# Weights asked for ahead of a stage's end, and h read back by ranges of tokens, in a two-block float32 network on one core

## The chip, the cores and the metric

The kernel runs on one core of one Trainium2 chip. Its time is device microseconds of one execution; the median of several runs is given. The engines are PE (matrix multiply), DVE (vector), ACT (scalar), POOL (general) and SP, which here only issues transfers. All five run their own instruction streams and meet by semaphores.

## The reference

Two transformer-like blocks over 1024 tokens of width 1024, with 256 context tokens before them, all in float32. The first block mixes a gated delta rule (GDN) and retention, multiplies each by a silu gate, projects, and ends with a gated feed-forward part. The second has a state-space branch and two attention branches, each multiplied by a sigmoid gate and merged.

```
h = concat([modulate(rms_norm(ctx)), modulate(rms_norm(x))])      # 1280 tokens x 1024
p = h @ w_in                                                      # qkv, z, ab | rq, rk, rv, rg
o_gdn = rms_norm(o_f + o_b) * silu(z)                             # "gate 1"
rq, rk = rope(rq), rope(rk) * d**-0.5
o_ret = group_norm(r_f + r_b) * silu(rg)                          # "gate 2"
x = x + g1 * (concat([o_gdn, o_ret]) @ w_out)                     # first output projection
x = x + g2 * swiglu(modulate(rms_norm(x)))
# second block
m = sigmoid(ga)*(ya @ w_oa) + sigmoid(gb)*(ys @ w_ob) + sigmoid(gc)*(yc @ w_oc)
x = x + gate1 * (m @ w_out_2);  x = x + gate2 * conv_ffn(...)
```

## The kernel before

The program is a row of stages in a fixed order, the same on every engine: GDN projections and scan (`gp`, `gs`), gate 1 (`gg1`), retention projections (`rp`), retention scan (`rs`), means and gate 2 (`rg`, `gg2`), first output projection (`op1`), first feed-forward (`ffn1`), state space (`sx`, `sc_`, `sz`), merge 0, attention 1 with merge 1 (`att1`, `mg1`), attention 2 with merge 2 (`att2`, `mg2`), second output projection and feed-forward. At the start of a stage an engine passes `barrier(e, stage)`, which waits until all engines have finished what the stage before counts on its semaphores, since the SBUF of one stage is given to the next.

Activations lie with the width on the partitions: h is 8 blocks of 128 rows by 1280 tokens, one after another in a partition, with the context tokens first. The latent tokens are worked on in two ranges, `LAT = [(0, 512), (512, 512)]`; over all tokens the ranges are `ALL = [(0, 256), (256, 512), (768, 512)]`. h is 5 MB and is stored to HBM (`hspill`) in the first stage. It is read back into SBUF twice: for gate 1 and the retention projections (`hT2`), and for gate 2 (`hT3`), at the same address; both transfers are issued by POOL, after the barrier.

Weights come in blocks of 256 columns (1 MB with 8 blocks of 128 rows) into two slots, `wslot0` and `wslot1`, taken in turn. `load()` on SP waits until the slot is given back by the last reader of its former block (`slots.give`), and then issues. SP goes through all loads and stores of the kernel in program order, so a wait on SP holds everything behind it, and a barrier that stands ahead of a load holds the load.

In a gate (`Gate`) PE first does the sums of squares of a head (`norm`), then for each of 4 tiles of 128 columns and both token ranges 8 products of h with weights; ACT applies silu, DVE multiplies. In gate 1 and `rp` each tile also carries a piece of the adaLN modulation (`at1`: weights asked for by POOL, multiplied by POOL, reduced by DVE, summed by PE). In `rp`, PE does a tile, and one tile later rotates its copy, which ACT has taken out of PSUM (`raw`); ahead of its first copy ACT computes decay tables. `op1` uses weights and activations split into a high and a low part (`woh`, `wol`, `op1yh`, `op1yl`): ACT writes the high part, DVE the rest; PE does three products for each. DVE waits for x (`x1_in`) when it has split y, and before it splits the second column of weights.

In attention each of two head groups (`AttGroup`) computes 8 gate tiles beside its scores and stores them to HBM (`gspill`, on SP, each when ACT has copied it); the merge reads them back (`gr`), applies the sigmoid and multiplies them with the branch's products. Merges 1 and 2 have 4 weight blocks "o" of 512 KB each.

Of the kernel before, what the change touches and what calls it, by code (L numbers as in the profile page):

```python
# [96 lines left out]
def build(nc, io, out):  # L97
# [238 lines left out]
    class Ada:  # L336
# [7 lines left out]
        def sp(self, e, g):  # L344
            load(e, (self.nm, g), [(self.w, 0, 8, g * 256, 256, 0)])
# [1147 lines left out]
    class Gate:  # L1493
# [41 lines left out]
        def pe(self, e):  # L1535
            st = self.st

            def norm(x):
                for n0, n in LAT:
                    b = self.bk.take("norm", x, n0)  # L1540
                    for ev in self.bk.freed("norm", x, n0):
                        e.wait_ge(*ev)
                    e.wait_ge(*st.act.after("sq", x, n0))
                    e.matmul(b[:, 0:n], ones, self.sq[:, self.at(x, n0, n)]).then_inc(st.pe("norm", x, n0), 1)
            norm(0)
            for ev in self.ready:
                e.wait_ge(*ev())
            for m in range(4):
                e.wait_ge(*loaded(self.nm, m // 2))
                s = slots[self.nm, m // 2]  # L1550
                for n0, n in LAT:
                    b = self.bk.take("mm", m, n0)
                    for ev in self.bk.freed("mm", m, n0):
                        e.wait_ge(*ev)
                    product(e, b[:, 0:n], [(wtile(s, k, m % 2 * 128), self.h(k, CT + n0, n)) for k in range(8)]).then_inc(st.pe("mm", m, n0), 1)
                    if self.tiles:
                        self.tiles.pe(e, m * 2 + n0 // 512)
                    if n0 == 0 and m < 3:
# [35 lines left out]
    drop(m0)  # L1594
    drop(m2, "right")
    hT2 = sb("hT2", [8 * TT])
    h2_in = Sem("hT2", 16)
    (hb, hbc) = views(hT2)
    bk_r = Ring(bank)
    at1 = AdaTiles("at1", [(ad1, m, 0) for m in range(16, 40)], bk_r, [sb(f"at1w{i}", [1024]) for i in range(3)])  # L1600
    mg = mark()
    gg1 = Gate("gate1", 1536, hb, yg, "gdn_norm_g", lambda x, n0: [], [lambda: h2_in.after("in")])
    gg1.bk, gg1.tiles = bk_r, at1
    drop(mg)

    def gate1_sp(e):
        gg1.sp(e)
# [13 lines left out]
    def gate1_pool(e):  # L1621
        barrier(e, gs)
        e.wait_ge(*hs_out.after("out"))
        e.dma_start(hT2[:, :], io["hspill"]).then_inc(h2_in("in"), 16)
        at1.pool(e, range(9))


# [14 lines left out]
    RT = [(0, m, n0, n) for m in range(4) for n0, n in ALL[1:]] + [(1, m, n0, n) for m in range(4) for n0, n in ALL]  # L1642

    def rp_sp(e):
        barrier(e, gg1.st)
        e.dma_start(rope1[:, :], io["rope1"]).then_inc(rope1_in("in"), 16)
        for g in range(6):
            load(e, ("rqkv", g), [(w1, 0, 8, RQ + g * 256, 256, 0)])

    def rp_dst(kind, m, n0, n):  # L1650
# [4 lines left out]

    def rp_pe(e):
        barrier(e, gg1.st)
        e.wait_ge(*h2_in.after("in"))

        def rotate(t):  # L1660
            kind, m, n0, n = t
# [282 lines left out]
    yr = rb("yr", [4 * NL])  # L1944
    m3 = mark()
    hT3 = sb("hT3", [8 * TT])
    h3_in = Sem("hT3", 16)
    (hd3, _) = views(hT3)
    rg = Stage("rg", rp)
    gg2 = Gate("gate2", 3600, hd3, yr, "ret_norm_g", lambda x, n0: [rg.dve.after("c", x, n0)], [lambda: h3_in.after("in")])  # L1950
    bk_g = gg2.bk
    drop(m0)

# [26 lines left out]

    def rg_pool(e):
        barrier(e, rs)
        e.dma_start(hT3[:, :], io["hspill"]).then_inc(h3_in("in"), 16)


    rsx = sb("rsx", [NL])
# [120 lines left out]
    class OutProj:  # L2107
# [6 lines left out]
            self.bk = Ring(bank[0:6])  # L2114
            self.xs = halves(self.yh, self.yl)

        def sp(self, e):
            for g in range(4):
                load(e, (self.nm, g), [(self.w, 0, 8, g * 256, 256, 0)])

        def cut_act(self, e, j):
# [69 lines left out]
    drop(0, "right")  # L2191

    def op1_sp(e):
        barrier(e, gg2.st)
        e.dma_start(x1[:, :].rearrange("p (k t) -> p k t", t=NL), io["xT"]).then_inc(x1_in("in"), 16)
        op1.sp(e)

    def op1_act(e):
        barrier(e, gg2.st)
# [975 lines left out]
    class Merge:  # L3175
# [10 lines left out]

        def sp(self, e):
            if self.att:
                for x in self.att.g_out:
                    e.wait_ge(*x.now())  # L3190
                barrier(e, *self.before)
            for g in range(4):
                if self.att:
                    for m, n0, n in self.blocks[g * 4:g * 4 + 4]:
                        gb = self.gr.take(m, n0)
                        for ev in self.gr.freed(m, n0):
                            e.wait_ge(*ev)
                        e.dma_start(gb[:, 0:n], io["gspill"][:, m * NL + n0:m * NL + n0 + n]).then_inc(self.gate_in(m, n0)(self.br, m, n0), 16)
                    load(e, (self.nm, "o", g), [(self.wo, 0, self.kt, g * 256, 256, 0)])
                else:  # L3200
                    for q in (0, 1) if g == 0 else (g + 1,) if g < 3 else ():
                        load(e, (self.nm, "g", q), [(w2, 0, 8, self.col + q * 256, 256, 0)])
                    load(e, (self.nm, "o", g), [(self.wo, 0, self.kt, g * 256, 256, 0)])

        def tiles_pe(self, e, kind, g, there=lambda n0: []):
            st, bk = self.st, self.bk
# [78 lines left out]
    class AttGroup:  # L3285
# [85 lines left out]
            e.activation(b[:, :], self.bg[m, n0][:, :], AF.Copy).then_inc(self.st.act("g", m, n0), 1)  # L3371
            self.bg.give((m, n0), self.st.act.now())

        def gate_sp(self, e):
            for b in range(8):
                m, n0 = self.gate(b)
                if b == 4:
                    load(e, (self.nm, "g", m // 2), [(w2, 0, 8, self.at.gcol + m * 128, 256, 0)])
                e.wait_ge(*(self.sj if b < self.early else self.st).act.after("g", m, n0))
                out_ = self.at.g_out[b % 3]  # L3380
                e.dma_start(io["gspill"][:, m * NL + n0:m * NL + n0 + 512], self.gs[m, n0][:, :]).then_inc(out_(self.at.br, m, n0), 16)
                self.gs.give((m, n0), out_.now())


        def sp(self, e):
            g = self.g
            load(e, (self.nm, "k"), [(w2, 0, 8, self.at.k0 + 64 * g, 64, 64 * x) for x in range(2)])
            load(e, (self.nm, "q"), [(w2, 0, 8, self.at.q0 + g * 256, 256, 0)])
            load(e, (self.nm, "g", g * 2), [(w2, 0, 8, self.at.gcol + g * 512, 256, 0)])
            self.gate_sp(e)  # L3390

        def lags(self, j):

# [314 lines left out]
    class Attention:  # L3708
# [19 lines left out]
        def yk(self, k, n0, n):  # L3728
            return self.y[:, k * NL + n0:k * NL + n0 + n]

        def sp(self, e):
            load(e, ("v", self.br), [(w2, 0, 8, self.v0, 128, 0)])
            for gr in self.groups:
                gr.sp(e)

        def pe(self, e):
            barrier(e, *self.before)
# [138 lines left out]
    def sp(e):  # L3876
        a_sp(e)
        gp_sp(e)
        gs_sp(e)
        gate1_sp(e)  # L3880
        rp_sp(e)
        rg_sp(e)
        op1_sp(e)
        ffn1_sp(e)
        fn_sp(e)
        sx[0].sp(e, 0)
        sx[0].sp(e, 1)
# [11 lines left out]
        op2.sp(e)  # L3899
        ffn2.sp(e)  # L3900
        last_sp(e)

# [164 lines left out]
```

## Time and profile before

| | before |
|---|---|
| median of 3 runs | 4852.59 us (4849.14 to 4853.21) |
| the profiled execution's own time | 4851.07 us |
| its span in the trace | 4849.1 us |
| PE busy | 4374.9 us, 90% of the span |
| mean granted clock of PE | 0.948 of full |
| DVE, ACT, POOL busy | 2341.2, 1394.8, 965.8 us |
| chain that ended last | PE 61%, DVE 9%, ACT 5%, DMA 1% |

The span is what the trace covers; the profiled execution took 2.0 us more than it. Times below are microseconds from the span's start. The time in brackets behind a row of a timeline is how long the engine had stood idle before it, and who released it.

### The profile page before, as it was taken

How to read it: one execution, taken by the hardware profiler on the slowest of the kernel's cores; microseconds unless marked ns; L12 is line 12 of the kernel's file. 1: busy time of each engine (PE TensorE's matmuls, PEld its weight loads, DVE VectorE, ACT ScalarE, POOL GpSimd, SP SyncE). 2: the span in 40 equal slices, each digit the busy share in tenths (PEclk: the TensorE clock that was granted, in tenths of full speed). 3: DMA queues.
4: the chain of work that ended last, by engine and by line, in shares of the span. 5: the costliest groups of instructions: out<-in, count | busy, mean ns of one | idle time of the engine just before them, and what ended most of it. 6: DMA issues, size and time to landing. Idle time of an engine off the chain costs nothing.

```text
span 4849.1 us, 45136 instructions
## 1 busy us (share of the span) xinstructions
PE 4374.9 (90%) x18128; PEld 3029.8 (62%) x18128; DVE 2341.2 (48%) x3763; ACT 1394.8 (29%) x2615; POOL 965.8 (20%) x743
## 2 busy tenths in 40 slices
PE   7895789988999999988889998989888888999998
PEld 3454754756788888645554455555564647888886
DVE  2768974252555563335442017563666644333334
ACT  2462221122211111332311005351453532222222
POOL 0114634121344441025241000002000011000001
PEclk9997899999999999988889999999999999999999
DMA  5112233112233431120211110112000031111111
GB/s 187 36 63 72 81 124 108 38 44 87 79 113 109 122 109 48 67 71 27 70 34 35 36 43 22 31 48 61 20 20 16 20 112 37 53 44 50 46 44 61
DMA packets 253617, 301.47 MB, mean 62 GB/s; under 512 B 18992, under 2 KB 209856, under 8 KB 251872
## 3 DMA queue, kind: packets, MB, share of 16 engines
q1 hardware_dynamic: 234976, 216.66, 14.6%
q0 software_dynamic: 15312, 76.68, 5.0%
q10 hardware_dynamic: 3120, 5.24, 0.3%
q8 instruction: 143, 2.34, 0.2%
q14 instruction: 66, 0.54, 0.0%
HBM read 268.47 MB, written 30.09 MB: 62 GB/s over the span
## 4 chain that ended last, share of the span: by engine, by line
PE 61%; DVE 9%; ACT 5%; DMA 1%; issue 1%; POOL 1%; SPq 0%; POOLq 0%; DVEq 0%; ACTq 0%
PE bank L193 59%; PE bank L196 2%; DVE Mx L205 1%; ACT Mx L202 1%; ACT at21P L202 1%; ACT at20P L202 1%; DVE at21sm L223 1%; POOL sq L205 1%; DVE at20sm L223 1%; DVE x L211 0%; DMA wslot<-in_w_in 0%; DVE wfl L205 0%; DVE at11sm L223 0%; DMA hT<-hspill 0%; DVE at21Pl L205 0%
## 5 line engine op out<-in xcount | busy, mean ns | idle before, releaser
L193 PE MATMUL bank<-h,wslot 128*128 128x512 f32 (+3 forms) x2096 | 899.5, 573 | 32.9 <-DMA wslot<-in_w_in 19.2
L193 PEld LDWEIGHTS bank<-h,wslot 128*128 128x128 f32 (+1 forms) x2096 | 383.8, 191 | 378.7 <-issue 361.2
L193 PE MATMUL bank<-hT,wslot 128*128 128x512 f32 (+3 forms) x1136 | 466.0, 567 | 36.6 <-DMA hT<-hspill 20.1
L193 PEld LDWEIGHTS bank<-hT,wslot 128*128 128x128 f32 (+1 forms) x1136 | 213.7, 191 | 264.7 <-issue 237.9
L193 PE MATMUL bank<-ffn1h,wfh 128*128 128x512 f32 x704 | 280.0, 398 | 11.4 <-DVE ffn1l L211 10.6
L193 PE MATMUL bank<-ffn2h,wgh 128*128 128x512 f32 x704 | 276.5, 393 | 9.7 <-DVE ffn2l L211 9.2
L211 DVE SCALAR_TENSOR_TENSOR x<-bank,mod,x 128x512 f32<-128x512 f32 x224 | 164.4, 746 | 247.0 <-PE bank L193 246.7
L193 PE MATMUL bank<-ffn1l,wfh 128*128 128x512 f32 x704 | 275.3, 391 | 0.0
L193 PE MATMUL bank<-ffn2l,wgh 128*128 128x512 f32 x704 | 274.9, 390 | 0.0
L193 PE MATMUL bank<-ffn1h,wfl 128*128 128x512 f32 x704 | 274.7, 390 | 0.0
L193 PE MATMUL bank<-ffn2h,wgl 128*128 128x512 f32 x704 | 274.7, 390 | 0.0
L205 DVE TENSOR_TENSOR wfl<-wslot,wfh 128x1024 fp32r<-128x1024 f32 (+2 forms) x92 | 151.0, 1642 | 149.6 <-ACT wfh L202 149.6
L205 POOL TENSOR_TENSOR ffn2al<-ffn2ga,ffn2ah 128x512 fp32r<-128x512 f32 x44 | 57.4, 1305 | 655.3 <-ACT ffn2ah L202 655.3
L226 DVE TENSOR_REDUCE at2a<-ffn1t 128x128 f32<-128x1024 f32 x72 | 143.1, 1988 | 44.2 <-POOL ffn1t L205 44.2
L193 PEld LDWEIGHTS bank<-ffn1h,wfh 128*128 128x128 f32 x704 | 132.6, 188 | 44.2 <-DVE ffn1l L211 10.2
L193 PEld LDWEIGHTS bank<-ffn2h,wgh 128*128 128x128 f32 x704 | 132.5, 188 | 43.2 <-DVE ffn2l L211 10.2
L211 DVE SCALAR_TENSOR_TENSOR ffn2ga<-ffn2gw,par,ffn2ga 128x1024 f32<-128x1024 f32 x44 | 56.5, 1285 | 199.5 <-ACT ffn2ga L202 198.7
L205 POOL TENSOR_TENSOR sq<-sq 128x512 f32<-128x512 f32 x56 | 71.7, 1280 | 397.0 <-ACT sq L202 395.1
L193 PEld LDWEIGHTS bank<-ffn1h,wfl 128*128 128x128 f32 x704 | 132.8, 189 | 28.0
L193 PEld LDWEIGHTS bank<-ffn2h,wgl 128*128 128x128 f32 x704 | 132.7, 189 | 27.7
L193 PEld LDWEIGHTS bank<-ffn2l,wgh 128*128 128x128 f32 x704 | 132.7, 189 | 26.8
L193 PEld LDWEIGHTS bank<-ffn1l,wfh 128*128 128x128 f32 x704 | 132.9, 189 | 25.4
(533 smaller groups left out, 8867.6 us busy)
## 6 DMA issues: line engine op xcount, KB each, us to landing
wslot<-in_w_in SPq DMA_DIRECT2D x40, 1024.0 KB, 5.5
ffn1t<-in_w_mod POOLq DMA_DIRECT2D x64, 512.0 KB, 4.8
wslot<-in_w_ffn_in SPq DMA_DIRECT2D x44, 512.0 KB, 5.4
Mx<-acsT SPq DMA_DIRECT2D x32, 512.0 KB, 4.9
at1w<-in_ada_w POOLq DMA_DIRECT2D x24, 512.0 KB, 4.6
wslot<-in_ffn_w_gate SPq DMA_DIRECT2D x22, 512.0 KB, 4.0
wslot<-in_ffn_w_up SPq DMA_DIRECT2D x22, 512.0 KB, 5.3
hT<-hspill POOLq DMA_DIRECT2D x2, 5120.0 KB, 15.3
```

The lines of the kernel that those rows point to most:

```text
L193: return Counted() if counting[0] else self.q.matmul(o, l, r, start=start, stop=stop)
L196: return Counted() if counting[0] else self.q.transpose(o, i, ident)
L202: return Counted() if counting[0] else self.q.activation(o, i, f, **k)
L205: return Counted() if counting[0] else self.q.tensor_tensor(o, a, b, op)
L211: return Counted() if counting[0] else self.q.scalar_tensor_tensor(o, a, s, b, op0, op1)
L223: return Counted() if counting[0] else self.q.reduce_max(o, a, AX.X)
L226: return Counted() if counting[0] else self.q.reduce_sum(o, a, AX.X)
```

## The change

Five edits. (1) h is read back in one transfer for each range of tokens, each with a semaphore of its own, the ranges of latent tokens first; the gates' PE waits for a range only when it comes to it, and the second reading leaves the context tokens out. (2) In `rp_sp` the first two weight blocks are asked for ahead of the barrier and of the table of cosines. (3) In `op1_sp` two of four blocks are asked for ahead of the barrier and of x. (4) In an attention, the next user's first block (the key weights of the second head group, or the merge's first block) is asked for ahead of the store of the seventh gate tile. (5) The merge asks for its second block before it waits for the stores and the barrier.

```diff
 class Gate, pe():
             norm(0)
-            for ev in self.ready:
-                e.wait_ge(*ev())
             for m in range(4):
                 e.wait_ge(*loaded(self.nm, m // 2))
                 s = slots[self.nm, m // 2]
                 for n0, n in LAT:
+                    e.wait_ge(*self.ready(n0))
                     b = self.bk.take("mm", m, n0)
...
-    h2_in = Sem("hT2", 16)
+    h2_in = [Sem(f"hT2{i}", 16) for i in range(3)]
+    def by_token(a, n0, n):
+        return a.rearrange("p (k t) -> p k t", t=TT)[:, :, n0:n0 + n]
...
     def gate1_pool(e):
         barrier(e, gs)
         e.wait_ge(*hs_out.after("out"))
-        e.dma_start(hT2[:, :], io["hspill"]).then_inc(h2_in("in"), 16)
+        for i, (n0, n) in enumerate([ALL[1], ALL[2], ALL[0]]):
+            e.dma_start(by_token(hT2[:, :], n0, n), by_token(io["hspill"], n0, n)).then_inc(h2_in[i]("in"), 16)
         at1.pool(e, range(9))
...
     def rp_sp(e):
-        barrier(e, gg1.st)
-        e.dma_start(rope1[:, :], io["rope1"]).then_inc(rope1_in("in"), 16)
         for g in range(6):
+            if g == 2:
+                barrier(e, gg1.st)
+                e.dma_start(rope1[:, :], io["rope1"]).then_inc(rope1_in("in"), 16)
             load(e, ("rqkv", g), [(w1, 0, 8, RQ + g * 256, 256, 0)])
...
     def rg_pool(e):
         barrier(e, rs)
-        e.dma_start(hT3[:, :], io["hspill"]).then_inc(h3_in("in"), 16)
+        for i, (n0, n) in enumerate(ALL[1:]):
+            e.dma_start(by_token(hT3[:, :], n0, n), by_token(io["hspill"], n0, n)).then_inc(h2_in[i]("again"), 16)
...
     def op1_sp(e):
+        op1.sp(e, (0, 1))
         barrier(e, gg2.st)
         e.dma_start(x1[:, :].rearrange("p (k t) -> p k t", t=NL), io["xT"]).then_inc(x1_in("in"), 16)
-        op1.sp(e)
+        op1.sp(e, (2, 3))
...
 class Merge, sp():
             if self.att:
+                self.o_sp(e, 1)
                 for x in self.att.g_out:
                     e.wait_ge(*x.now())
                 barrier(e, *self.before)
@@
-                    load(e, (self.nm, "o", g), [(self.wo, 0, self.kt, g * 256, 256, 0)])
+                    if g >= 2:
+                        self.o_sp(e, g)
...
+        def o_sp(self, e, g):
+            load(e, (self.nm, "o", g), [(self.wo, 0, self.kt, g * 256, 256, 0)])
...
-        def gate_sp(self, e):
+        def gate_sp(self, e, ahead):
             for b in range(8):
                 m, n0 = self.gate(b)
+                if b == 6:
+                    ahead(e)
                 if b == 4:
                     load(...)
...
 class Attention:
-        def sp(self, e):
+        def sp(self, e, ahead):
             load(e, ("v", self.br), [(w2, 0, 8, self.v0, 128, 0)])
-            for gr in self.groups:
-                gr.sp(e)
+            self.groups[0].k_sp(e)
+            self.groups[0].sp(e, self.groups[1].k_sp)
+            self.groups[1].sp(e, ahead)
...
-        att1.sp(e)
+        att1.sp(e, lambda e: mg1.o_sp(e, 0))
         mg1.sp(e)
-        att2.sp(e)
+        att2.sp(e, lambda e: mg2.o_sp(e, 0))
```

On POOL at the start of gate 1, `kd` and `vb` being the end of the GDN scan and `at1w` the adaLN weights:

```order
 L205 TENSOR_TENSOR kd<-kb,kdf 128x512
 L205 TENSOR_TENSOR vb<-vb,bet 128x512
-L232 DMA hT<-hspill 128x10240
+L232 DMA hT<-hspill 128x8x512 x2
+L232 DMA hT<-hspill 128x8x256
 L232 DMA at1w<-in_ada_w 128x8x128 x3
 L205 TENSOR_TENSOR at1w<-at1w,sc 128x1024
```

One transfer has become three, and the adaLN loads stand behind all of them.

On SP from gate 1 to the first output projection; `in_w_in` are the weights of the projections, `in_w_out` those of the output projection, `rope` the table, `x` the residual:

```order
 L232 DMA wslot<-in_w_in 128x8x256 x2
-L232 DMA rope<-in_rope 128x2560 [waits s_gate1_dve,s_gate1_act,s_gate1_pe]
-L232 DMA wslot<-in_w_in 128x8x256 x2
+L232 DMA wslot<-in_w_in 128x8x256 [waits s_gate1_pe] x2
+L232 DMA rope<-in_rope 128x2560 [waits s_gate1_dve,s_gate1_act]
 L232 DMA wslot<-in_w_in 128x8x256 [waits s_rp_pe] x6
-L232 DMA x<-in_xT 128x8192 [waits s_gate2_dve,s_gate2_act,s_gate2_pe]
-L232 DMA wslot<-in_w_out 128x8x256 x2
+L232 DMA wslot<-in_w_out 128x8x256 [waits s_gate2_pe] x2
+L232 DMA x<-in_xT 128x8192 [waits s_gate2_dve,s_gate2_act]
 L232 DMA wslot<-in_w_out 128x8x256 [waits s_op1_dve] x2
```

The table and x have moved behind two weight loads each, and those now wait for PE alone.

On SP at the end of the first attention's second group, with `gspill` the stores of gate tiles, `gr` their reading back and `in_w_oa` the merge's weights:

```order
-L232 DMA gspill<-sq 128x512 [waits s_at11j_act] x4
+L232 DMA gspill<-sq 128x512 [waits s_at11j_act] x2
+L232 DMA wslot<-in_w_oa 128x4x256 [waits s_at11j_pe]
+L232 DMA gspill<-sq 128x512 [waits s_at11j_act] x2
+L232 DMA wslot<-in_w_oa 128x4x256 [waits s_at11j_pe]
 L232 DMA gr<-gspill 128x512 [waits s_at11j_pe,s_at11j_act,s_gout2,s_at11j_dve,s_gout1,s_gout0]
-L232 DMA gr<-gspill 128x512 x3
-L232 DMA wslot<-in_w_oa 128x4x256
-L232 DMA gr<-gspill 128x512 x4
-L232 DMA wslot<-in_w_oa 128x4x256
+L232 DMA gr<-gspill 128x512 x7
```

Both weight loads have moved ahead of the first `gr`, the one that waits for the barrier; the second attention has the same rows with `in_w_oc`.

## Rows read from the trace of the kernel before

**Rows 1.** Page, part 1: busy time of PE, share of the span, instructions.
```profile
PE 4374.9 (90%) x18128; PEld 3029.8 (62%) x18128; DVE 2341.2 (48%) x3763; ACT 1394.8 (29%) x2615; POOL 965.8 (20%) x743
```

**Rows 2.** PE's waits, whole span: us in total, times, longest.
```profile
PE bank L193 <- DMA wslot<-in_w_in: 31.2, 5, 12.0
...
PE bank L193 <- DVE wol L205: 19.0, 1, 19.0
```

**Rows 3.** Timeline of PE, gate 1 into retention: start, us, what, idle before.
```profile
663.14 8.89 PE L193 MATMUL bank<-hT,wslot 128*128 128x512 f32 x16 [13.23 <-DMA hT<-hspill]
...
728.98 0.28 PE L193 MATMUL bank<-cst,at1a 128*128 128x1 f32 x2
741.27 15.93 PE L193 MATMUL bank<-hT,wslot 128*128 128x512 f32 x32 [12.01 <-DMA wslot<-in_w_in]
757.04 1.02 PE L193 MATMUL bank<-rr,cst 128*128 128x512 f32 x2
```

**Rows 4.** Timeline of POOL, gate 1.
```profile
647.66 0.59 POOL L232 DMA_DIRECT2D hT<-hspill  x1 [13.31 <-DVE yg L205]
648.24 2.67 POOL L232 DMA_DIRECT2D at1w<-in_ada_w  x3
664.98 1.89 POOL L205 TENSOR_TENSOR at1w<-at1w,sc 128x1024 f32<-128x1024 f32 x1 [14.07 <-DMA at1w<-in_ada_w]
```

**Rows 5.** Page, part 6: issues, KB each, us from issue to landing.
```profile
hT<-hspill POOLq DMA_DIRECT2D x2, 5120.0 KB, 15.3
...
x<-in_xT SPq DMA_DIRECT2D x1, 4096.0 KB, 12.1
...
ro<-in_rope POOLq DMA_DIRECT2D x2, 1024.0 KB, 5.9
```

**Rows 6.** Timeline of DVE, end of gate 1.
```profile
729.81 0.69 DVE L205 TENSOR_TENSOR yg<-yg,sgate 128x512 f32<-128x512 f32 x1 [2.98 <-ACT sgate L202]
```

**Rows 7.** Timeline of ACT, start of retention.
```profile
745.98 0.28 ACT L202 ACTIVATE zt<-cst,lg 128x1 f32<-128x1 f32 x1
750.37 0.60 ACT L202 ACTIVATE rr<-bank 128x512 f32<-128x512 f32 x1 [4.11 <-PE bank L193]
```

**Rows 8.** Timeline of POOL, start of gate 2.
```profile
1022.42 0.60 POOL L232 DMA_DIRECT2D hT<-hspill  x1 [10.03 <-ACT yl L202]
```

**Rows 9.** Timeline of PE, gate 2.
```profile
1028.96 1.88 PE L193 MATMUL bank<-sqgate,cst 128*128 128x512 f32 x4
1037.67 9.36 PE L193 MATMUL bank<-hT,wslot 128*128 128x512 f32 x16 [6.83 <-DMA hT<-hspill]
...
1048.58 13.90 PE L193 MATMUL bank<-hT,wslot 128*128 128x512 f32 x32
```

**Rows 10.** Timelines of ACT and DVE, start of the first output projection.
```profile
1116.81 1.06 ACT L202 ACTIVATE woh<-wslot 128x1024 fp32r<-128x1024 f32 x1 [13.97 <-DMA wslot<-in_w_out]
...
1127.47 1.22 DVE L205 TENSOR_TENSOR wol<-wslot,woh 128x1024 fp32r<-128x1024 f32 x1
```

**Rows 11.** Timeline of SP, start of merges 1 and 2.
```profile
3259.75 1.74 SPq L232 DMA_DIRECT2D gr<-gspill  x4
...
3913.36 1.74 SPq L232 DMA_DIRECT2D gr<-gspill  x4
```

**Rows 12.** The chain that ended last: start, us, what.
```profile
1127.01 82.59 PE bank L193 x363
...
3268.18 56.62 PE bank L193 x128
...
3921.46 57.66 PE bank L193 x128
```

**Rows 13.** Windows of PE: us, busy (instructions), granted clock, DMA share, GB/s.
```profile
3258.00:3260.00 2.00, 0.17 (x2) 1.00 0.00 0
...
3264.00:3268.00 4.00, 0.00 (x0) 0.50 0.96 302
...
3911.50:3913.50 2.00, 0.28 (x2) 1.00 0.00 0
```

More of the change, by code:

```diff
@@ L1601, in build @@
     mg = mark()
-    gg1 = Gate("gate1", 1536, hb, yg, "gdn_norm_g", lambda x, n0: [], [lambda: h2_in.after("in")])
+    gg1 = Gate("gate1", 1536, hb, yg, "gdn_norm_g", lambda x, n0: [], lambda n0: h2_in[n0 // 512].after("in"))
     gg1.bk, gg1.tiles = bk_r, at1
     drop(mg)
+    def by_token(a, n0, n):
+        return a.rearrange("p (k t) -> p k t", t=TT)[:, :, n0:n0 + n]
     def gate1_sp(e):
@@ L1657, in rp_pe @@
         barrier(e, gg1.st)
-        e.wait_ge(*h2_in.after("in"))
+        for x in h2_in:
+            e.wait_ge(*x.after("in"))
         def rotate(t):
@@ L1946, in build @@
     hT3 = sb("hT3", [8 * TT])
-    h3_in = Sem("hT3", 16)
     (hd3, _) = views(hT3)
     rg = Stage("rg", rp)
-    gg2 = Gate("gate2", 3600, hd3, yr, "ret_norm_g", lambda x, n0: [rg.dve.after("c", x, n0)], [lambda: h3_in.after("in")])
+    gg2 = Gate("gate2", 3600, hd3, yr, "ret_norm_g", lambda x, n0: [rg.dve.after("c", x, n0)], lambda n0: h2_in[n0 // 512].after("again"))
     bk_g = gg2.bk
@@ L2115, in __init__, with sp @@
             self.xs = halves(self.yh, self.yl)
-        def sp(self, e):
-            for g in range(4):
+        def sp(self, e, groups):
+            for g in groups:
                 load(e, (self.nm, g), [(self.w, 0, 8, g * 256, 256, 0)])
@@ L3202, in sp @@
                         load(e, (self.nm, "g", q), [(w2, 0, 8, self.col + q * 256, 256, 0)])
-                    load(e, (self.nm, "o", g), [(self.wo, 0, self.kt, g * 256, 256, 0)])
+                    self.o_sp(e, g)
+        def o_sp(self, e, g):
+            load(e, (self.nm, "o", g), [(self.wo, 0, self.kt, g * 256, 256, 0)])
         def tiles_pe(self, e, kind, g, there=lambda n0: []):
@@ L3382, in gate_sp, with k_sp @@
                 self.gs.give((m, n0), out_.now())
-        def sp(self, e):
+        def k_sp(self, e):
+            load(e, (self.nm, "k"), [(w2, 0, 8, self.at.k0 + 64 * self.g, 64, 64 * x) for x in range(2)])
+        def sp(self, e, ahead):
             g = self.g
-            load(e, (self.nm, "k"), [(w2, 0, 8, self.at.k0 + 64 * g, 64, 64 * x) for x in range(2)])
             load(e, (self.nm, "q"), [(w2, 0, 8, self.at.q0 + g * 256, 256, 0)])
             load(e, (self.nm, "g", g * 2), [(w2, 0, 8, self.at.gcol + g * 512, 256, 0)])
-            self.gate_sp(e)
+            self.gate_sp(e, ahead)
         def lags(self, j):
@@ L3729, in yk, with sp @@
             return self.y[:, k * NL + n0:k * NL + n0 + n]
-        def sp(self, e):
+        def sp(self, e, ahead):
             load(e, ("v", self.br), [(w2, 0, 8, self.v0, 128, 0)])
-            for gr in self.groups:
-                gr.sp(e)
+            self.groups[0].k_sp(e)
+            self.groups[0].sp(e, self.groups[1].k_sp)
+            self.groups[1].sp(e, ahead)
         def pe(self, e):
@@ L3894, in sp @@
         mg0.sp(e)
-        att1.sp(e)
+        att1.sp(e, lambda e: mg1.o_sp(e, 0))
         mg1.sp(e)
-        att2.sp(e)
+        att2.sp(e, lambda e: mg2.o_sp(e, 0))
         mg2.sp(e)
-        op2.sp(e)
+        op2.sp(e, range(4))
         ffn2.sp(e)
```

## The prediction

> **What bounds the kernel now.** I read the table of PE's waits first, then the timelines of PE, POOL, SP, DVE and ACT around each stage boundary that the diff touches, then the granted clock there. The program is a row of stages, each ended by a barrier that every engine passes, and within most of them the tensor engine (PE) runs without a gap; so a microsecond of PE idleness at a boundary is a microsecond of the span; PE is busy 90% of it [rows 1]. The reader is to see in the waits that weights of the next stage stand high: those from the input projection 31.2 us in 5 waits, the first output projection's split weights 19.0 in one [rows 2]. Of the 31.2, one wait of 12.01 stands at the start of the retention projections [rows 3]; the other four are not at a place that the diff moves. The timelines add the two waits for h, 13.23 and 6.83 us [rows 3, 9], and the chain the starts of the two merges [rows 12].
>
> **The change part by part.** Six places can give time; each is costed by when PE (or the engine it waits for) can start in place of when it did.
>
> *Gate 1, h by ranges.* POOL asks for h at 647.66, the transfer of 5120 KB takes 15.3 us to land [rows 4, 5], and PE starts at 663.14 after 13.23 us idle [rows 3]. After the change PE needs only the first 2048 KB. No such load is in the trace from POOL; the nearest are 1024 KB in 5.9 us and 5120 KB in 15.3 us [rows 5], and the straight line between them gives 5.9 + 9.4/4 = 8.25 us. So PE starts at 647.66 + 8.25 + 0.18 (the 0.18 that stood between landing and start before) = 656.1: 7.0 us. The ranges land in the order asked for, I take it, because the adaLN tile that POOL asked for 0.6 us behind h was used only at 664.98, 2 us after h had landed, though it is a tenth of the size [rows 4]. The second range, 4.7 us later by the same line, is there before the first product of that range, which stands behind a first half-tile of 7 us and more. POOL now issues three DMAs before the adaLN tiles: a load of 1024 short rows costs it 0.89 us (three in 2.67) against 0.59 for the one it replaces, so the tiles are asked for 2.1 us later [rows 4]. The first of them feeds a DVE reduction in the gate's own chain; as it lies behind the same 5 MB either way, I take 0.5 off, with 0 and 2.1 as bounds. **6.5 us**; bounds 0 (no range earlier than the whole) and 9.4 (a range as quick as the 5.9 us load).
>
> The Trainium skill (DMA: Bandwidth & Descriptors, Anatomy of one DMA) gives a fixed 2.0 us and 436 KB per us for a POOL transfer; by it the first range would land in 6.8 us as an estimate, and the sum below would be 1.4 us larger, all of it at gate 1. The measured pair of rows is slower than that fit, and the measured pair is what I use.
>
> *Retention, weights before the barrier.* PE finishes gate 1's products at 729.0 and waits 12.01 us, until 741.27, for weights that SP asked for behind the barrier and behind the cosine table [rows 3]. Now the first block of weights is asked for when gate 1's first block is free, some 30 us ahead, and the barrier alone stands before PE: it is met when DVE's last product of the gate ends, 729.81 + 0.69 = 730.5 [rows 6]. What is late next is ACT: it computes decay tables from the same barrier on, up to 745.98 + 0.28, and only then copies PE's first tile out (0.60 us) [rows 7]. PE does its two first tiles in 13.9 us (a warm 32 products, [rows 9]), until 744.5, and waits for that copy until 746.8, where before it went on at 757.04 [rows 3]. **10.2 us**. The second block now stands ahead of the table in SP's queue; the table has from 730.6 to 746 to land, and 1280 KB in front of or behind 1024 KB need less than the 15.3 us of 5120 KB. Bounds 9 and 10.7.
>
> *Gate 2.* POOL asks at 1022.42 [rows 8]; PE is done with means and norms at 1028.96 + 1.88 = 1030.84 and waits until 1037.67, 6.83 us [rows 9]. The first range lands at 1022.42 + 8.25 + 0.18 = 1030.85: the wait is gone. The idle also let PE's clock fall: the first 16 products took 9.36 us where 32 warm ones took 13.90 [rows 9], 2.4 us more than half of it. With no gap that goes too. **9.2 us**; bounds 2.0 (the two ranges land together, at the line's 13.0 us for 4096 KB, so that PE starts at 1035.6, and slowly) and 9.2.
>
> *First output projection.* SP asked for x (4096 KB, 12.1 us to land [rows 5]) before the weights; ACT stood 13.97 us waiting for them before it could split the first column [rows 10]. Now two blocks of weights are asked for ahead of the barrier, the first of them at half of gate 2, so ACT splits at once, and everything behind, DVE's splitting of y included, moves up by the same. **14.0 us.** What is queued behind the moved load: x now stands behind 1024 KB of weights. DVE waits for x before its part of the split of column 1, which takes 1.22 us and stood at 1127.47, now 1113.5 [rows 10]. x, asked for at 1101.7, lands at 1113.8 alone and at 1117.0 as the last of 5120 KB in 15.3 us; PE has work in column 0 until 1127.01 - 14.0 + 27 products of 0.23 (82.59 over 363) = 1119.2 [rows 12], so x costs nothing up to 1118.0. Bounds 11 and 14.2.
>
> *Merges.* SP passes the barrier at 3259.75 and 3913.36 and asks for four gate tiles before the weights [rows 11]; PE starts at 3268.18 and 3921.46 [rows 12]. With both blocks of weights there, PE starts at the barrier: 8.4 and 8.1 us. The granted clock is still at 1.00 (2.4 GHz) in the 2 us around both barriers, and at 0.50 (1.2 GHz) only later in the wait [rows 13], and PE's 128 products took 56.62 and 57.66 us [rows 12], where four times the warm 32 are 55.6: another 1.0 and 2.1 for a start without the fall. **9.4 and 10.2 us.** PE has eight banks, so the gate tiles, now asked for when PE starts, hold it up only if they are eight products late. Bounds 7.5 and 11 each.
>
> *Nothing.* The key weights of the second head group, asked for two stores earlier, are not among PE's waits at that place; the stores behind them wait only if the slot is not free, and it has been free since four gate tiles earlier. Retention's other loads keep their place behind PE's release of a slot.
>
> **Sum:** 6.5 + 10.2 + 9.2 + 14.0 + 9.4 + 10.2 = 59.5 us off the profiled execution's 4851.07, that is 4791.6; the median of the runs is 1.5 higher, so 4793.1.
>
> Of the fall of the clock the trace shows both ends, 1.00 when a wait begins and 0.50 late in it [rows 13]. The Trainium skill (TensorE: Matmul & The Clock Gate, the part on the HAM clock gate) says that an idle array drops to 1.2 GHz and needs activity to be released. By that rule, and the rows agree, the 5.5 us of these terms that are clock (2.4, 1.0 and 2.1) come back with the waits; a reading of busy time alone would leave the sum at 54 and the time at 4798.6.
>
> **The rivals.**
> *A, the ranges don't come in order* (they share the queue, or 2 KB rows are slower than the 40 KB rows of before). For it: no load of this shape from POOL is in the trace. Against: the adaLN tile's landing. Gate 1 gives 0, gate 2 gives 2.0: 59.5 - 6.5 - 7.2 = 45.8, time 4806.8.
> *B, x takes the place of the weights* in the output projection. For it: x stands behind another 1024 KB now. It decides from a landing at 1118.0, which is 16.3 us after its issue; at 5 us later the time is 4798.
> *C, slower than before.* One mechanism: with the idle gone PE is loaded more evenly and the mean granted clock falls. PE is busy 4375 us [rows 1] at a mean clock of 0.948 (the table of times); 60 us are lost when the mean falls to 0.935. For it: the mean is under 1 already, with the engine busy 90% of the span. Against: the falls that I looked at stand inside waits. At 0.93 the time would be 4878.
> *D, the merges' terms do not come,* since the SP queue stops at the load put ahead of the stores: that needs the slot's last reader to be later than the sixth store. It would cost the 19.6 us: 4812.7.
>
> **How the numbers follow.** My forecast, all six terms within their own bounds (4786 to 4801), 68 in 100; A 14; B 9; D 4; C with any cause of no gain 5. The likeliest gives 4793.1. The range from 4784 to 4812 takes in the forecast, A and B, and the lower bounds of two terms at once; it leaves out C and D. A measurement of this kernel tells about 0.2% (10 us) from no change. C is the only case that is not faster by more: slower 0.02, same 0.02, faster 0.96.
>
> **What would show it.** Right: PE's wait for h near 6 us at gate 1 and under 1 at gate 2; retention's first tile at the barrier and then a wait of some 2 us for ACT's copy; no wait of ACT for output weights; both merges starting within 0.3 us of SP's gate loads, at full clock. Wrong: h waits of 10 us and more (A), DVE waiting for x (B), SP held at a weight load before the sixth store (D), or a mean clock under 0.94 (C).

## The result, and the profile after

The changed kernel takes 4799.22 us (median of 4 runs, 4796.0 to 4800.64), beside 4850.86 us for the kernel before on the same chip (4848.49 to 4853.21). The ratio is 0.9888 with an interval of 0.9876 to 0.99, that is 51.6 us less. The forecast was 4793.1; what came is 6 us above it and inside the likeliest case's own range of 4786 to 4801. The profiled execution took 4797.95 us with a span of 4796.1, 53.0 us less than before; the mean granted clock is 0.953 (0.948 before).

The page's first part, against [rows 1], and PE's waits, against [rows 2]: 31.2 us for the projections' weights have become 19.2, h has fallen to one wait, the split weights from 19.0 to 5.0.

```profile
PE 4370.5 (91%) x18128; PEld 3031.7 (63%) x18128; DVE 2342.6 (49%) x3763; ACT 1395.5 (29%) x2615; POOL 971.0 (20%) x746
```

```profile
PE bank L193 <- DMA wslot<-in_w_in: 19.2, 4, 5.2
...
PE bank L193 <- DVE y L205: 7.0, 4, 1.8
PE bank L193 <- DMA hT<-hspill: 6.9, 1, 6.9
...
PE bank L193 <- DVE wol L205: 5.0, 1, 5.0
```

The timeline of PE at the six places, against [rows 3, 9, 12]:

```profile
656.26 9.74 PE L193 MATMUL bank<-hT,wslot 128*128 128x512 f32 x16 [6.93 <-DMA hT<-hspill]
...
682.77 0.35 PE L193 MATMUL bank<-cst,at1a 128*128 128x1 f32 x2 [1.10 <-DVE at1a L226]
...
717.11 7.11 PE L193 MATMUL bank<-hT,wslot 128*128 128x512 f32 x16
...
725.82 13.97 PE L193 MATMUL bank<-hT,wslot 128*128 128x512 f32 x32 [1.49 <-ACT sgate L202]
741.91 1.12 PE L193 MATMUL bank<-rr,cst 128*128 128x512 f32 x2 [2.12 <-ACT rr L202]
...
743.01 8.81 PE L193 MATMUL bank<-hT,wslot 128*128 128x512 f32 x16
...
1017.77 7.11 PE L193 MATMUL bank<-hT,wslot 128*128 128x512 f32 x16 [0.27 <-issue]
...
1083.05 0.77 PE L193 MATMUL bank<-op1yh,woh 128*128 128x512 f32 x1 [4.95 <-DVE wol L205]
...
3223.98 55.17 PE L193 MATMUL bank<-y,wslot 128*128 128x512 f32 x128 [1.75 <-DVE y L205]
3281.55 19.73 PE L193 MATMUL bank<-wslot,h 128*128 128x128 f32 x160 [2.40 <-POOL mT L205]
...
3870.84 55.17 PE L193 MATMUL bank<-y,wslot 128*128 128x512 f32 x128 [1.75 <-DVE y L205]
```

The reader is to see how one place is read after the other, by how far PE stands ahead of the kernel before: POOL asks for h 0.56 us earlier by chance (647.10), retention's first rotation starts 15.13 us earlier (757.04, [rows 3]), gate 2's second norm 22.14 (1024.72, and 1046.86 in the kernel before), and the last merge 50.6 (3921.46, [rows 12]). Both merges start at the barrier, and their 128 products take the time of a warm engine. POOL at gate 1, against [rows 4]:

```profile
647.10 2.72 POOL L232 DMA_DIRECT2D hT<-hspill  x3 [13.33 <-DVE yg L205]
649.80 2.65 POOL L232 DMA_DIRECT2D at1w<-in_ada_w  x3
666.47 1.90 POOL L205 TENSOR_TENSOR at1w<-at1w,sc 128x1024 f32<-128x1024 f32 x1 [14.02 <-DMA at1w<-in_ada_w]
```

The landing times of the transfers of h, the five ranges and the first store; for the ranges [rows 5] had one transfer of 5120 KB in 15.3 us:

```profile
DMA to landing us min/median/max: 8.6/13.3/15.7
```

Taken alone, the first range lands 9.0 us after its own request at gate 1 and 8.6 at gate 2:

```profile
DMA to landing us min/median/max: 9.0/9.0/9.0
...
DMA to landing us min/median/max: 8.6/8.6/8.6
```

The second ranges land 13.5 and 13.1 us after their own requests, the context tokens' range 15.7. At gate 1 the three are there 9.0, 14.5 and 17.5 us after POOL's first request; the one transfer of before was there after 15.4.

SP at the first merge, against [rows 11]: the two weight blocks stand ahead of the barrier, and the gate tiles are asked for 0.17 us before PE starts.

```profile
3179.40 0.43 SPq L232 DMA_DIRECT2D wslot<-in_w_oa  x1
...
3211.11 0.43 SPq L232 DMA_DIRECT2D wslot<-in_w_oa  x1
3223.81 3.64 SPq L232 DMA_DIRECT2D gr<-gspill  x8
```

ACT and DVE at the output projection, against [rows 10]. ACT splits the first column of weights as soon as it has copied y; DVE is held 2.32 us by x before the second column, and PE is not held by it.

```profile
1080.61 1.04 ACT L202 ACTIVATE woh<-wslot 128x1024 fp32r<-128x1024 f32 x1
```

```profile
1093.65 1.23 DVE L205 TENSOR_TENSOR wol<-wslot,woh 128x1024 fp32r<-128x1024 f32 x1 [2.32 <-DMA x<-in_xT]
```

| term | forecast | from the positions |
|---|---|---|
| chance, ahead of every edit | 0 | 0.6 |
| gate 1 | 6.5 | 4.4 |
| retention | 10.2 | 10.2, less 1.8 for a fall of the clock |
| gate 2 | 9.2 | 8.8 |
| output projection | 14.0 | 14.1 |
| merge 1 | 9.4 | 9.6, less 1.6 for a fall of the clock |
| merge 2 | 10.2 | 10.4 |
| stages that no edit touches | 0 | -1.6 |
| sum | 59.5 | 53.1 |

### The profile page after: what moved, and what is told of

Read it like the earlier page. It is cut to its first block, busy times and chain, and to the rows that moved or that the text cites. A ratio compares the mean times of both kernels' runs of the same rounds, so it can differ in the third digit from the quotient of the medians.

```text
span 4796.1 us, 45140 instructions
## 1 busy us (share of the span) xinstructions
PE 4370.5 (91%) x18128; PEld 3031.7 (63%) x18128; DVE 2342.6 (49%) x3763; ACT 1395.5 (29%) x2615; POOL 971.0 (20%) x746
## 4 chain that ended last, share of the span: by engine, by line
PE 62%; DVE 9%; ACT 5%; POOL 1%; issue 1%; DMA 1%; POOLq 0%; DVEq 0%; ACTq 0%
PE bank L193 60%; PE bank L196 2%; DVE Mx L205 1%; ACT at21P L202 1%; ACT at20P L202 1%; ACT Mx L202 1%; DVE at21sm L223 1%; POOL sq L205 1%; DVE at20sm L223 1%; DVE x L211 0%; DMA wslot<-in_w_in 0%; DVE wfl L205 0%; DVE at11sm L223 0%; DVE at21Pl L205 0%; DVE at10sm L223 0%
## 5 line engine op out<-in xcount | busy, mean ns | idle before, releaser
L193 PE MATMUL bank<-h,wslot 128*128 128x512 f32 (+3 forms) x2096 | 896.9, 572 | 32.9 <-DMA wslot<-in_w_in 19.2
L193 PE MATMUL bank<-hT,wslot 128*128 128x512 f32 (+3 forms) x1136 | 462.6, 564 | 13.7 <-DMA hT<-hspill 6.9
L193 PE MATMUL bank<-ffn1h,wfh 128*128 128x512 f32 x704 | 280.6, 399 | 10.2 <-DVE ffn1l L211 9.4
L193 PEld LDWEIGHTS bank<-ffn2h,wgh 128*128 128x128 f32 x704 | 132.6, 188 | 43.2 <-DVE ffn2l L211 10.2
```

The costliest lines, as they stand in the source:

```text
L193: return Counted() if counting[0] else self.q.matmul(o, l, r, start=start, stop=stop)
```

## The experiments

Each was run beside the kernel before. The first four do one part of the change alone; the others change the changed kernel. The times of one part are small beside what differs between two executions elsewhere, so each verdict rests on the distance between two instructions that enclose the edit, with the median beside it.

**h by ranges alone** (all of edit 1, nothing else).

```diff
-        e.dma_start(hT2[:, :], io["hspill"]).then_inc(h2_in("in"), 16)
+        for i, (n0, n) in enumerate([ALL[1], ALL[2], ALL[0]]):
+            e.dma_start(by_token(hT2[:, :], n0, n), by_token(io["hspill"], n0, n)).then_inc(h2_in[i]("in"), 16)
...
-        e.dma_start(hT3[:, :], io["hspill"]).then_inc(h3_in("in"), 16)
+        for i, (n0, n) in enumerate(ALL[1:]):
```

> The kernel before with h read by ranges alone, weights as before. Theory (terms add, each at its own boundary; 4.4 us at gate 1 and 8.8 at gate 2 in the changed kernel's profile): 13 us below the kernel before, 10 to 16. Rival (the range reads are worth less without the early weights, since the weights' wait then takes their place): gate 2 as in theory, but gate 1's gain goes into a longer wait for retention's weights, 9 us below. The profile tells: the wait for weights at the start of retention stays at 12 us in the theory and becomes 16 in the rival.

Measured: 4842.04 us (4834.65 to 4845.2), ratio 0.9975 (0.9964 to 0.9986), median 10.5 us under that of the kernel before. PE's timeline:

```profile
655.90 10.05 PE L193 MATMUL bank<-hT,wslot 128*128 128x512 f32 x16 [6.92 <-DMA hT<-hspill]
...
736.31 15.97 PE L193 MATMUL bank<-hT,wslot 128*128 128x512 f32 x32 [12.32 <-DMA wslot<-in_w_in]
...
1026.38 7.10 PE L193 MATMUL bank<-hT,wslot 128*128 128x512 f32 x16 [0.48 <-issue]
```

The wait for weights in retention stays at 12.3, so the gain of gate 1 isn't swallowed there, as the rival would have it. From POOL's request to the gate's last 16 products it is 70.02 us, 74.37 before: 4.4 for gate 1 (4.35), not 6.5. From the second request to the first product of the output projection it is 8.6 less: gate 2. The two add to the 13 that the theory expected, and the median shows 10.5 of them. The first product of that projection stands 13.6 us earlier than in the kernel before (1105.7 for 1119.3), of which only 8.4 are left at the end. The edit doesn't touch the stages between: from the last scores of attention 1's first head group to the first of attention 2's it is 378.3 us, 373.1 before. Why is open.

**Retention's weights alone** (edit 2).

```diff
-        barrier(e, gg1.st)
-        e.dma_start(rope1[:, :], io["rope1"]).then_inc(rope1_in("in"), 16)
         for g in range(6):
+            if g == 2:
+                barrier(e, gg1.st)
+                e.dma_start(rope1[:, :], io["rope1"]).then_inc(rope1_in("in"), 16)
```

> The kernel before with the first two retention blocks of weights ahead of the barrier and the table, nothing else. Theory: PE's 12 us wait is replaced by 1.5 us for the barrier and 2.1 us for ACT's copy, 10.2 us, of which a fall of PE's clock in that 2.1 us wait takes back 1.8: 8.4 us below. Rival (the fall of the clock in the changed kernel was chance of that one execution): 10.2 us below and a granted clock of 1.00 behind the wait.

Measured: 4844.3 us (4838.15 to 4848.97), ratio 0.9981 (0.9972 to 0.9991), median 8.2 us less. PE's timeline:

```profile
749.39 1.12 PE L193 MATMUL bank<-rr,cst 128*128 128x512 f32 x2 [2.10 <-ACT rr L202]
...
750.49 7.11 PE L193 MATMUL bank<-hT,wslot 128*128 128x512 f32 x16
```

From POOL's request to this rotation it is 9.1 us less than before, with 1.2 us more for gate 1's first 16 products (10.06 for 8.89, where no edit was), so 10.2 for the edit. The same wait of 2.1 us as in the changed kernel is followed by products at full speed: the fall of the clock isn't a consequence of the edit that always comes. In this trace the rival came, not the theory. The median, 8.2, would fit the theory's 8.4 better, but the ten runs lie up to 10.8 us apart and can't decide between 8.4 and 10.2.

**The output projection alone** (edit 3).

```diff
+        op1.sp(e, (0, 1))
         barrier(e, gg2.st)
...
-        op1.sp(e)
+        op1.sp(e, (2, 3))
```

> The kernel before with two blocks of output weights ahead of the barrier and of x, nothing else. Theory: ACT's 13.97 us wait goes, 14.1 us below, and the wait of DVE for x (2.3 us in the changed kernel) costs PE nothing. Rival (DVE's wait for x does reach PE): 12 us below, and PE waits for the split of column 1.

Measured: 4838.04 us (4835.75 to 4842.17), ratio 0.9969 (0.9957 to 0.9981), median 14.5 us less, span 14.1 less. PE starts at 1104.55 in place of 1119.27, and POOL had asked for h 0.6 us earlier: 14.1.

**The merges alone** (edits 4 and 5).

```diff
+                self.o_sp(e, 1)
                 for x in self.att.g_out:
                     e.wait_ge(*x.now())
                 barrier(e, *self.before)
...
-        att1.sp(e)
+        att1.sp(e, lambda e: mg1.o_sp(e, 0))
...
-        att2.sp(e)
+        att2.sp(e, lambda e: mg2.o_sp(e, 0))
```

> The kernel before with the early loads of attention and merges alone (key weights of the second group, first and second block of both merges). Theory: 9.4 and 10.2 us, together 19.6 below, of which 16.5 are the earlier starts and 3 the clock that doesn't fall. Rival (the clock part is given back in the stage behind, as the 1.6 us in the changed kernel's second attention suggest): 16.5 to 17 us below.

Measured: 4831.87 us (4828.68 to 4833.27), ratio 0.9957 (0.994 to 0.9973), median 20.7 us less. From attention 1 to attention 2 (last scores of the one's first head group, 3048.3, to the first of the other, 3411.3) 363.0 us pass, 373.1 before: 10.1; the second merge 10.4 in the same way. Attention 2's first 160 products take 18.10 us, as in the kernel before, not the 19.73 of the changed kernel's profile.

The four medians add to 10.5 + 8.2 + 14.5 + 20.7 = 53.9 us, the four edits together gave 51.6: the parts neither help nor hide one another by more than the few us by which such medians differ.

**The changed kernel again**, as the yardstick for three variants on the same chip.

> The changed kernel once more, as the yardstick for three variants of it on the same chip. Nothing is edited. Both theories: about 4799 us (4796 to 4801), 52 us under the kernel before. What is asked of its trace: after PE's 2.1 us wait for ACT's copy in retention, does PE's clock fall (16 products in 8.8 us, as in its first profile) or not (7.1 us, as in the kernel with the retention edit alone). If the fall hangs on the wait alone, it is there again; if it hangs on how the moment happens to fall, either can be seen, and the spans of two profiles of the same program can differ by some 2 us.

Measured: 4799.1 us (4797.33 to 4800.92), ratio 0.9888 (0.9873 to 0.9903). The clock falls again behind the wait of 2.1 us (8.52 us for the 16 products), but attention 2 starts with 18.10 us in place of 19.73. Two profiles of one program differ on the way by more than at the end: the line of the state space's first products, of the first profile and of this one, shows 3.3 us between them (2125.0 and 2128.3), though their spans differ by 0.6 us at the end.

```profile
L193 PE MATMUL bank<-xt,Mx x512: 275/421/447, 2125.0 to 2450.2; 128*128 128x64 f32 x171
```

```profile
L193 PE MATMUL bank<-xt,Mx x512: 274/294/447, 2128.3 to 2451.9; 128*128 128x64 f32 x171
```

**The adaLN tiles between the ranges.**

```diff
-        for i, (n0, n) in enumerate([ALL[1], ALL[2], ALL[0]]):
+        def part(i, n0, n):
             e.dma_start(by_token(hT2[:, :], n0, n), by_token(io["hspill"], n0, n)).then_inc(h2_in[i]("in"), 16)
-        at1.pool(e, range(9))
+        part(0, *ALL[1])
+        at1.fetch(e, 0)
+        part(1, *ALL[2])
+        at1.pool(e, range(1), False)
+        part(2, *ALL[0])
+        at1.pool(e, range(1, 9))
```

The call with `False` multiplies the first tile without asking for it again, and asks for the two tiles behind it.

> The changed kernel with POOL's issues at gate 1 in another order: first range of h, first adaLN tile, second range, two more tiles, the first multiplication, and only then the context tokens' range. Theory: gate 1 gave 4.4 us in place of 6.5 since the adaLN tile was asked for 2.1 us later, behind three issues, and the gate's chain of products waits for its reduction on DVE. Then the last product of the gate ends at about 723 in place of 724.9 and the time is 1.5 to 2 us under that of the changed kernel beside it; PE's first product of h stays at 656. Rival: the two us were lost between PE's first products and the DVE operation that took 2.3 us beside POOL's multiplication, whatever the order; then the end of the gate moves by under 0.5 us and the time is the same.

Measured: 4792.49 us (4790.65 to 4795.52), ratio 0.9875 (0.986 to 0.989); 6.6 us less than the changed kernel beside it, with runs that don't overlap. POOL's timeline at gate 1, then PE's:

```profile
647.13 0.96 POOL L232 DMA_DIRECT2D hT<-hspill  x1 [13.33 <-DVE yg L205]
648.09 0.90 POOL L232 DMA_DIRECT2D at1w<-in_ada_w  x1
648.97 0.88 POOL L232 DMA_DIRECT2D hT<-hspill  x1
...
657.65 1.90 POOL L205 TENSOR_TENSOR at1w<-at1w,sc 128x1024 f32<-128x1024 f32 x1 [6.03 <-DMA at1w<-in_ada_w]
```

```profile
655.94 8.79 PE L193 MATMUL bank<-hT,wslot 128*128 128x512 f32 x16 [6.57 <-DMA hT<-hspill]
...
723.40 13.97 PE L193 MATMUL bank<-hT,wslot 128*128 128x512 f32 x32 [1.46 <-ACT sgate L202]
739.53 1.12 PE L193 MATMUL bank<-rr,cst 128*128 128x512 f32 x2 [2.15 <-ACT rr L202]
...
740.63 7.11 PE L193 MATMUL bank<-hT,wslot 128*128 128x512 f32 x16
```

PE starts as it did, the wait for `at1a` is gone, and from POOL's request to retention's start it takes 1.9 us less than in the yardstick (76.3 for 78.2): the theory's size, from the tile's place. Its reason, the later request, isn't shown by it (see gate 1 below), since the move also takes the tile from behind three transfers of h to behind one. Another 1.7 is the clock, which did not fall this time behind the same 2.15 us. The other 3 us of the median are not the edit's by any row that I found.

**ACT's first copy earlier.**

```diff
             e.activation(dtmp[1][:, :], C("dB"), AF.Exp, scale=lg[:, 4 + x:5 + x]).then_inc(rp.act("d1", x), 1)
+        rp_raw(e, RT[0])
...
-            raw(t)
+            if j:
+                raw(t)
```

`rp_raw` is the copy that `raw` makes, written once more; it now stands behind the four tables `Dk` and ahead of the eight pairs `xi` and `zt`.

> The changed kernel with ACT's first copy of a retention tile moved from behind the last decay tables to the middle of them. Theory: PE's wait of 2.1 us at 741.9 is ACT's alone, and with it goes the fall of the clock behind it (16 products in 8.8 us, 7.1 warm) where that is seen: 2.1 us less than the changed kernel beside it, up to 4 with the clock. Rival: the tables and the copy are needed at the same place anyway (DVE's rotation waits for what ACT computes later), so PE waits just as long one tile later, and the time is the same.

Measured: 4791.8 us (4791.01 to 4793.46), ratio 0.9874 (0.9858 to 0.9891); 7.3 us less than the yardstick. ACT's timeline, then PE's:

```profile
734.77 0.57 ACT L202 ACTIVATE rr<-bank 128x512 f32<-128x512 f32 x1
735.24 0.39 ACT L202 ACTIVATE xi<-cst,lg 128x128 f32<-128x128 f32 x1
...
738.88 0.28 ACT L202 ACTIVATE zt<-cst,lg 128x1 f32<-128x1 f32 x1
739.07 0.57 ACT L202 ACTIVATE rr<-bank 128x512 f32<-128x512 f32 x1
```

```profile
723.09 13.97 PE L193 MATMUL bank<-hT,wslot 128*128 128x512 f32 x32 [1.45 <-ACT sgate L202]
736.90 1.02 PE L193 MATMUL bank<-rr,cst 128*128 128x512 f32 x2
```

PE goes from its second tile to the rotation without a gap: 2.1 us less, and 1.8 for the clock up to gate 2. The rival falls. A further 3.0 us of this profile is chance, since POOL asks for h at 644.8 where the yardstick's does at 647.8.

**Both.** No new line: the two edits above together.

> The changed kernel with both edits: adaLN tiles between the ranges, and ACT's first copy earlier. Theory: the two gains add, 3.6 to 6 us under the changed kernel beside it, about 4794 us. Rival: neither place bounds anything, and the time is that of the changed kernel within 1 us.

Measured: 4788.43 us (4784.01 to 4793.1), ratio 0.9866 (0.9851 to 0.9881), 10.7 us less than the yardstick and the fastest version here. From the request for h at gate 1 to the last one at gate 2 it is 356.5 us, 362.4 in the yardstick: 5.9, where 3.6 to 6 were expected. The medians show more than that; 5.4 us of the span lie behind gate 2, in stages that are word for word the same.

**The ranges in the other order.**

```diff
-        for i, (n0, n) in enumerate([ALL[1], ALL[2], ALL[0]]):
+        for i, (n0, n) in ((1, ALL[2]), (0, ALL[1]), (2, ALL[0])):
```

> The changed kernel with the second range of latent tokens asked for ahead of the first at gate 1 (gate 2 as changed). Theory, POOL's transfers land in the order in which they are asked for: the range that PE needs first now lands as the second, some 4.7 us later (13.3 us after the first issue in place of 8.6); PE's wait for h at gate 1 is about 11.6 us in place of 6.9, its first 16 products are slow in the same way, and the time is 4 to 5 us over that of the changed kernel (4803 to 4804). Rival, the ranges share the queue's bandwidth and land together or nearly: the wait stays within 1 us of 6.9 and the time is the same.

Measured: 4800.76 us (4797.85 to 4801.33), ratio 0.9892 (0.9876 to 0.9909). PE's timeline:

```profile
664.97 8.59 PE L193 MATMUL bank<-hT,wslot 128*128 128x512 f32 x16 [12.04 <-DMA hT<-hspill]
```

```profile
DMA to landing us min/median/max: 8.7/13.2/15.3
```

The wait is 12.04 us where order gives 11.6 and sharing 6.9: POOL's transfers land in the order asked. The price in time was expected at 4 to 5 us and is 2.8 in the trace (from the request to retention's start 81.55 us, 78.72 before the swap), since the later start also removes what the adaLN tile held up: its wait of 1.10 us is gone and the first products took 8.59 for 9.74. In the median of the runs it can't be told from nothing.

**The merge's first blocks behind the barrier, ahead of the gate tiles.**

```diff
-                self.o_sp(e, 1)
                 for x in self.att.g_out:
                     e.wait_ge(*x.now())
                 barrier(e, *self.before)
+                self.o_sp(e, 0)
+                self.o_sp(e, 1)
...
-        att1.sp(e, lambda e: mg1.o_sp(e, 0))
+        att1.sp(e, lambda e: None)
```

> The changed kernel with the first two weight blocks of merges 1 and 2 asked for behind the merge's barrier, but ahead of the eight gate tiles (before the change they stood behind the barrier and four and eight gate tiles). It parts the 19.6 us of the merges into what the barrier costs and what the place behind four gate loads costs. Theory: most is the barrier, since a 512 KB load asked for alone takes near 5 us to land; PE's first product then waits 5 to 6 us at each merge with a cold start of 1 to 2 us, and the time is 12 to 15 us over the changed kernel (4811 to 4814). Rival: the loads were late because four gate tiles stood ahead in SP's queue (1.74 us of issue and 1 MB of traffic); then a weight load asked for first lands in some 3 us and the time is only 5 to 8 us over the changed kernel.

Measured: 4808.83 us (4807.48 to 4810.56), ratio 0.9911 (0.9896 to 0.9925), 9.6 us over the changed kernel's median. SP's timeline, then PE's:

```profile
3225.06 0.93 SPq L232 DMA_DIRECT2D wslot<-in_w_oa  x2
3226.05 21.22 SPq L232 DMA_DIRECT2D gr<-gspill  x12
```

```profile
3228.63 57.34 PE L193 MATMUL bank<-y,wslot 128*128 128x512 f32 x128 [5.15 <-DMA wslot<-in_w_oa]
...
3878.90 58.17 PE L193 MATMUL bank<-y,wslot 128*128 128x512 f32 x128 [5.20 <-DMA wslot<-in_w_oc]
```

PE's wait is 5.15 and 5.20 us, and its products are slower by 2.2 and 3.0; by positions the merges cost 5.6 and 6.4 us more than where both blocks are early (368.9 for 363.3 from attention 1 to 2, 83.6 for 77.2 at the second). So of the 20 us that the merges gave, the barrier was worth 12 and the gate tiles ahead in SP's queue 8. Both explanations hold a share; the median lies between the two forecasts, 2.4 us under what the positions give. PE started 3.57 us after the block's request, so it landed within that, nearer to the rival's 3 than to the theory's 5.

## Why the prediction was right, and where its sizes were off

The mechanism held at all six places, though at gate 1 a tile that the prediction had put at 0.5 us set the pace; the rivals did not come. **A** (ranges out of order) falls by the landing times and by the swap. **B** (x in the weights' place): the wait of DVE that it named is there, 2.32 us, but x landed 14.1 us after its request, short of the 16.3 from which it would have decided, and PE's first product of the output projection stands 36.2 us ahead at its start and at the projection's end. **C** (evenly loaded, lower clock): the mean clock rose from 0.948 to 0.953. **D** (SP stopped): the load goes out 0.37 us behind the store ahead of it (3179.03 and 3179.40).

*Gate 1: 6.5, measured 4.4.* PE's start at 656.26, where 656.1 was said, is nearer than the reading behind it, by luck: POOL asked 0.56 us early. From the request PE starts after 9.16 us (15.48 before), where 8.43 were said, since the first range took 9.0 us to land and not 8.25; that is 6.3 us, not 7.0. The kernel before had a warning that the prediction left out: POOL's read of `x<-xspill`, 4096 KB, took 13.7 us, 0.7 over the straight line. But the start isn't what holds the gate, as the next number shows.

The step that was mis-sized is "as it lies behind the same 5 MB either way, I take 0.5 off, with 0 and 2.1 as bounds". POOL can use the adaLN tile 19.37 us after the request for h, 17.32 before: 2.05 us later, the upper bound. DVE's first reduction follows POOL's multiplication at 668.84, and DVE comes to the second one 11.90 us later (680.74), as in the kernel before (673.31 and 685.21, where the first waited for PE's products and not for the tile). So the tile now sets the gate's pace, and PE waits for the second reduction (1.10 <- DVE `at1a`), where before it did not at that place. The order with the tile between the ranges gave 1.9 us back, which shows that the tile's place is the cause.

Why the tile is late is not parted by any run. The prediction said POOL's later request: the tile is used some 16.7 us behind its own request in both kernels (648.24 to 664.98, 649.80 to 666.47). But that distance isn't fixed. The three tiles of the kernel before, asked for one after another, land 16.7, 17.6 and 18.3 us behind their own requests:

```profile
DMA to landing us min/median/max: 16.7/17.6/18.3
```

The other reading is that the three ranges take longer than the one transfer, 17.5 us for 15.4, and the tile follows 1.8 us behind the last of them in both kernels. By it a request put earlier gains nothing as long as the same transfers stand ahead. PE's slow first products cost little of the gate: in the last experiment they took 8.72 us, in the changed kernel 9.74, and the gate's last 16 products start 69.61 and 70.01 us after POOL's request.

*Retention: 10.2, measured 10.2.* The wait of some 2 us for ACT's copy was said and is there, 2.12, and moving the copy removes it. Not said was that PE's clock can fall behind it: the windows of PE (us, busy, granted clock in the column before the last two) show the clock at 0.75 and 0.68 where the retention edit alone had 1.00 in the windows at the same place.

```profile
742.00:745.00 3.00, 3.00 (x7) 1.47 (x8) 1.75 (x3) 0.34 (x1) 1.27 (x1) 0.75 0.00 0
745.00:748.00 3.00, 3.00 (x6) 1.24 (x5) 1.50 (x2) 0.00 (x0) 1.25 (x2) 0.68 0.00 0
```

```profile
749.00:752.00 3.00, 2.61 (x8) 1.42 (x9) 1.27 (x2) 0.82 (x2) 1.26 (x1) 1.00 0.00 0
```

*Gate 2: 9.2, measured 8.8,* with the first 16 products at 7.11 us: the 2.4 us of clock in the term came back. *Output projection: 14.0, measured 14.1.* *Merges: 9.4 and 10.2, measured 9.6 and 10.4,* with both sets of 128 products at 55.17. In the profile shown, 1.6 of the first was lost again behind it, since attention 2's first 160 products took 19.73 us after a wait of 2.40, where ten of the twelve profiles have 18.10 after the same wait (the other with 19.73 is that of ACT's first copy earlier).

*Nothing:* the key weights asked for earlier changed nothing, as said. The sum of 59.5 fell short by 6.4: 2.1 at gate 1, 3.4 in two falls of the clock, and 0.9 net in the small rows of the table; of the 1.6 lost in stages that the diff doesn't touch, 1.3 lie between attention 2's first scores and the last of its second head group (476.0 us, 474.7 before). A reading with the waits alone, 4798.6 in the prediction, lies closer to the measured 4799.2, but by chance: the clock terms it leaves out were all measured, and others went against them.

## What to carry to other kernels

A load that stands behind a barrier, or behind another load that is needed later, costs the engine that bounds nearly its whole latency, as the 14.1 us of the output projection show. Ask for it when its buffer is free, and look up with what it shares its queue: here splitting the transfer ahead of a small tile made the tile 2 us late, and the next chain hung on the small tile. Split a large read-back in the order of use. Measure an edit of some 10 us by the distance between two instructions that enclose it, not by the end of the span, which moves by 3 to 6 us without any edit.

## What was not expected of the hardware

**The same short wait does or doesn't cost clock.** PE stood idle for 2.10 to 2.17 us behind ACT's copy in six profiles, and the 16 products behind it took 8.81, 8.52 and 8.81 us in three profiles (the changed kernel twice, and the swapped ranges) and 7.11 in the other three (retention's weights alone, the adaLN tiles between, the merge behind its barrier). The Trainium skill (TensorE: Matmul & The Clock Gate, Part 1) says, of the products at a kernel's start, that how many run slow differs from run to run of one kernel, by the phase of the clock gate's monitor. This is a wait in mid-kernel, and the loss of 1.4 to 1.7 us in three profiles beside none in three is of the same kind; that it has the same cause isn't shown by any run here, and I leave it open; that the wait is needed for the fall is shown only so far as no fall was seen there in the two kernels without it.

**The first range of 2048 KB from POOL lands 9.0 us after its request at gate 1 and 8.6 at gate 2,** beside 8.25 by the straight line of the prediction. The Trainium skill (DMA: Bandwidth & Descriptors, Anatomy of one DMA) would make it 6.8 as an estimate; the measurement decides, and it is nearer to the line between this kernel's own rows.

**Ahead of every edit the programs differ.** POOL asks for h between 644.8 and 650.7 us in kernels that are the same up to there. That is as large as some of the terms. It may be why the medians of the last variants (6.6 and 7.3 us less) are larger than the 3.6 and 3.9 us that their rows account for; with one profile for each variant it isn't shown.
